# Hybrid decoder step: who loads the token forms at the passage from the up to the down projection, and when they are split

## The chip, the core and the metric

The kernel runs on one core of a Trainium2 chip. The metric is the time of one execution in microseconds (us), median of several runs; lower is better. TensorE multiplies matrices, VectorE (DVE) and ScalarE (ACT) do elementwise work, GpSimd (POOL) does some too, and SyncE (SP) only starts transfers. SP, ACT and POOL each have a queue of transfers (DMAs); all of them run on the same 16 DMA engines.

## The reference

One decoder layer for 592 token columns (16 meta tokens, 512 prompt tokens, 64 sample tokens). What matters here is the last step, a squared-ReLU MLP of width 8192 over a model width of 2048:

```
mix, c, sg, sh = token_mixer(rmsnorm(x), ...)
x = x + mix
u = relu(rmsnorm(x, norm2_w) @ w_up)      # (tokens, 2048) @ (2048, 8192)
x = x + (u * u) @ w_down                  # (tokens, 8192) @ (8192, 2048)
y = rmsnorm(x, final_norm_w)
```

All inputs and outputs are float32.

## The kernel before

The MLP works on 576 tokens as two halves of 288. Every block product of two by two is made with seven products instead of eight (a Strassen-like scheme), from sums of weight blocks and seven combinations of the activations, the *token forms* (`FORMS = 7`, numbered 0 to 6). Each operand is split into a high part (rounded) and a low part (the rest), and a product is 8 inner blocks times three matmuls: high by high, high weight by low form, low weight by high form. So one product is 24 matmuls of 128x128 by 288.

Seven products make a *pair*. There are 32 pairs of the up projection (`UP_PAIRS`, p = 0 to 31) and 32 of the down projection (p = 32 to 63). Below, (31,4) is product 4 of pair 31. Up pairs use token forms of x, down pairs use token forms of u*u, which the up pairs have made and stored, eight planes each, in DRAM (`u_forms`). Both live in the same buffers: `forms_a` holds forms 0 to 2, `forms_b` forms 3 to 6, each form a high and a low plane of 128 x 8 x 288. The passage is the replacement of the seven forms of x by the seven forms of the first eight up pairs, between pair 31 and pair 32. The buffer of form i is free when product (31,i), its last reader, has ended. After that 1.18 MB of it is loaded into the low plane (`load_form`), ACT rounds it into the high plane (`chunk_hi`, line 1728 of the profile), and DVE subtracts the high from the low plane in place, in two halves (`chunk_lo(i, half)`, line 2463).

Each engine runs its own instructions in the order written. DVE and ACT run through `slot(p, i)`, one slot for each product. A DVE slot takes the result of an earlier product (`take`, lines 2423 to 2445), makes the low part of the weights of product (p,i) (`mlp_lo`, line 2410, which waits until product i-2 has ended, since there are two buffers) and in some slots a weight sum (`weight_sum`, lines 2383, 2389, 2392, 2401) or forms of u (`u_forms`, lines 2452 to 2457); in the passage `chunk_lo` comes last in the slot. An ACT slot copies a result in slots 2 to 4 of up pairs (`copy_product`, line 1703), makes the high part of the weights of the next product (`mlp_hi`, line 1689), squares (`u_square`, line 1712), and in the passage does `chunk_hi` last. TensorE starts product (p,i) when `mlp_lo(p,i)` is done (`product_waits`); product (31,4) also waits for the copy of product (31,2); in pair 32 each product also waits for both halves of `chunk_lo(i)`.

Before the change SP's queue issues, in this order: weight blocks 128 to 130 (512 KB each; four blocks make a pair, block 4p + j), forms 0 and 1, blocks 131 and 132, form 2, the first tile of z (the running sum x that the down projection adds to, `load_z`), forms 3 and 4, block 133, forms 5 and 6. Each issue waits for its buffer and holds up those behind it. `weight_sum(32, 1)`, in DVE's slot (31,5), needs blocks 130 and 131. `load_z(32)` waits for POOL's store of the forms of pair 30 (`store_u(30)`), because z lies where they lay.

Of the kernel before, what the change touches and what calls it, by code (L numbers as in the profile page):

```python
# [21 lines left out]
F32 = mybir.dt.float32  # L22
F32R = mybir.dt.float32r
U8 = mybir.dt.uint8
ALU = mybir.AluOpType
ACT = mybir.ActivationFunctionType
# [29 lines left out]
KP = KT // 2  # L56
FORMS = 7
UP_PAIRS = DFF // P // 2
# [10 lines left out]
UB = [0, 1, 2, 4, 5, 6, 7]  # L69
# [14 lines left out]
F_ORDER = ([f"{i}_{k}" for k in range(KP - 1) for i in range(3)]  # L84
           + ["3a", "0_7", "1_7", "3b", "2_7", "4", "5a", "5b", "6"])
# [5 lines left out]
def unit_of(p, i):  # L91
    return MLP_U0 + FORMS * p + i
# [33 lines left out]


STEPS = PAIRS - UP_PAIRS
FIRST_FORMS = len(F_ORDER) + FORMS


def window(p):
# [4 lines left out]
def block_loads(n):  # L137

    p = n // 4
    return 2 if p >= UP_PAIRS and p - UP_PAIRS + KP > UP_PAIRS else 1  # L140


def block_count(n):

    return 16 * sum(block_loads(m) for m in range(n % BLOCKS, n + 1, BLOCKS))


def step_forms(t, group):

    return FIRST_FORMS + 2 * (t - 1) + 1 + group  # L150
# [83 lines left out]
def hymba_kernel(nc, io):  # L234
    ctx = ExitStack()
    with ctx:
# [160 lines left out]
        def form(i):  # L397

            f = forms_a[:, i] if i < 3 else forms_b[:, i - 3]
            return f[:, 0], f[:, 1]  # L400
# [46 lines left out]
        s_unit = sem("unit_done")  # L447
# [74 lines left out]
        def _(sp):  # L522
# [112 lines left out]
                    return  # L635
                sp.dma_start(wblock(n), src).then_inc(s_v[n % BLOCKS], 16)

            def load_form(i):

                sp.wait_ge(s_unit, unit_of(UP_PAIRS - 1, i) + 1)  # L640
                sp.wait_ge(s_ust[0], 16 * (KP // 2))
                sp.wait_ge(s_ust[1], 16 * (KP // 2))
                sp.dma_start(form(i)[1].bitcast(F32), u_dram[0:KP, UB[i]].rearrange("k p n -> p k n")).then_inc(s_fraw[i], 16)

            def load_z(p):
                d = p - UP_PAIRS
                if d < 2:
# [7 lines left out]
            for n in range(4 * PAIRS):  # L655
                load_block(n)
                p = n // 4 - 1 if n % 4 == 0 else PAIRS - 1 if n == 4 * PAIRS - 1 else 0
                for i in {4 * UP_PAIRS + 2: (0, 1), 4 * UP_PAIRS + 4: (2,)}.get(n, ()):
                    load_form(i)
                if p >= UP_PAIRS:  # L660
                    load_z(p)
                for i in {4 * UP_PAIRS + 4: (3, 4), 4 * UP_PAIRS + 5: (5, 6)}.get(n, ()):
                    load_form(i)

            sp.wait_ge(s_unit, unit_of(PAIRS - 1, 1) + 1)
            for r in range(2):
# [16 lines left out]
        def _(pool):  # L683
# [196 lines left out]
            def store_u(p):  # L880
                pool.wait_ge(s_uf, 3 * p + 3)
                pool.dma_start(u_dram[p].rearrange("f p n -> p f n"), ub[:, p % 2]).then_inc(s_ust[p % 2], 16)
# [14 lines left out]
                    pool.wait_ge(s_zf, 2 * e + 2)  # L897
                pool.dma_start(x1_dram[d % KP], z[:, p % 2]).then_inc(s_zst[p % 2], 16)

            for p in range(UP_PAIRS - 1):  # L900
                store_u(p)
            for p in range(UP_PAIRS - 1, PAIRS - 1):
                if p < UP_PAIRS:
                    store_u(p)
                else:
                    store_z(p)
# [46 lines left out]
        def _(pe):  # L953
# [331 lines left out]
            def part_product(p, i, ks):  # L1285

                f_hi, f_lo = form(i)
                u_ = unit_of(p, i)
                out = pbank(p, "abacaba"[i])
                t = p - UP_PAIRS  # L1290
                for k in ks:
                    if t > 0 and k == KP - 1 and i in (0, 3):
                        pe.wait_ge(s_flo, step_forms(t, i // 3))
                    if p == 0 and i < 3:
                        pe.wait_ge(s_flo, form_no(f"{i}_{k}"))
                    kx = k if t < 0 else window(p)[k] % KP
                    for n, (w, x) in enumerate(((hi_slot(u_), f_hi), (hi_slot(u_), f_lo), (w_lo[:, u_ % 2], f_hi))):
                        ins = mm(out, w[:, k, :], x[:, kx, :], start=i in (0, 1, 3) and k == 0 and n == 0,  # L1298
                                 stop=k == KP - 1 and n == 2, skip_group_check=True)
                    if k == KP - 1:  # L1300
                        ins.then_inc(s_unit, 1)

            def product_waits(p, i):
                pe.wait_ge(s_lo, unit_of(p, i) + 1)
                if i == 0:
                    if p < 2:
                        pe.wait_ge(s_evac, OUT_T0 + EARLY + KT - 1 + p)
                    else:
                        pe.wait_ge(s_ev, ev_end(p - 2))
                up = p < UP_PAIRS  # L1310
                if i == 2:
                    pe.wait_ge(s_tc, 3 * p + 1) if up else pe.wait_ge(s_ev, ev_no(p, 1))
                if i == 3 and p == 0:
                    pe.wait_ge(s_ws, 3)
                if i == 4:
                    pe.wait_ge(s_tc, 3 * p + 3) if up else pe.wait_ge(s_ev, ev_no(p, 3))
                if i == 6:
                    pe.wait_ge(s_ev, ev_no(p, 2 if up else 5))
                if p == UP_PAIRS:
                    pe.wait_ge(s_flo, len(F_ORDER) + i + 1)  # L1320
                if p == 0 and i >= 3:
                    pe.wait_ge(s_flo, form_no({3: "3b", 4: "4", 5: "5b", 6: "6"}[i]))

# [53 lines left out]
        def _(act):  # L1377
# [347 lines left out]
            def chunk_hi(i):  # L1725
                act.wait_ge(s_fraw[i], 16)
                f_hi, f_lo = form(i)
                A(f_hi, f_lo.bitcast(F32), ACT.Copy).then_inc(s_fhi, 1)

            def step_load(t, group):  # L1730

# [23 lines left out]
            def slot(p, i):  # L1755
                up = p < UP_PAIRS
                if up and 2 <= i <= 4:
                    copy_product(p, i - 2)
                if i < FORMS - 1:
                    mlp_hi(p, i + 1)  # L1760
                elif p + 1 < PAIRS:
                    mlp_hi(p + 1, 0)
                if p and i < 2:
                    if p - 1 < UP_PAIRS:
                        u_square(p - 1, i)
                    elif p - 1 >= PAIRS - KP:
                        z_finish(p - 1, i)
                t = p - UP_PAIRS
                if t == -1 and i >= 5:
                    chunk_hi(i - 5)  # L1770
                if t == 0 and i < 5:
                    chunk_hi(i + 2)
                if t == 0 and i == 4:
                    step_load(1, 0)
                if t == 0 and i == 6:
                    step_hi(1, 0)
                if t == 1 and i == 1:
                    step_load(1, 1)
                if t == 1 and i == 2:
                    step_hi(1, 1)  # L1780
                if t > 1 and i == 1:
                    step_hi(t, 1)
                if 0 < t < STEPS - 1:
                    if i == 0:
                        step_load(t + 1, 0)
                    if i == 3:
                        step_load(t + 1, 1)
                    if i == 4:
                        step_hi(t + 1, 0)
# [48 lines left out]
        def _(dve):  # L1838
# [620 lines left out]
            def chunk_lo(i, half):  # L2459
                f_hi, f_lo = form(i)  # L2460
                ks = slice(half * (KP // 2), (half + 1) * (KP // 2))
                dve.wait_ge(s_fhi, len(F_ORDER) + i + 1)
                ins = TT(f_lo[:, ks, :], f_lo[:, ks, :].bitcast(F32), f_hi[:, ks, :].bitcast(F32), ALU.subtract)  # L2463
                if half:
                    ins.then_inc(s_flo, 1)

            def step_lo(t, group):
                q = (t + KP - 1) % KP
# [6 lines left out]
            def slot(p, i):  # L2475
                if i >= 2:
                    take(p, i - 2)
                elif p:
                    take(p - 1, i + 5)
                mlp_lo(p, i)  # L2480
                if i == 1:
                    weight_sum(p, 3)
                if i == 3:
                    weight_sum(p, 4)
                if i >= 5 and p + 1 < PAIRS:
                    weight_sum(p + 1, i - 4)
                if 0 < p <= UP_PAIRS and i in (2, 4):
                    u_forms(p - 1, i // 2 - 1)
                t = p - UP_PAIRS
                if t == -1 and i == 6:  # L2490
                    chunk_lo(0, 0)
                if t == 0:
                    for f, half in {0: [(0, 1)], 1: [(1, 0), (1, 1)], 2: [(2, 0), (2, 1)], 3: [(3, 0), (3, 1)],
                                    4: [(4, 0), (4, 1)], 5: [(5, 0), (5, 1)], 6: [(6, 0), (6, 1)]}[i]:
                        chunk_lo(f, half)
                if t == 1 and i == 0:
                    step_lo(1, 0)
                if t == 1 and i == 3:
                    step_lo(1, 1)
                if t > 1 and i == 2:  # L2500
                    step_lo(t, 1)
                if 0 < t < STEPS - 1 and i == 4:
                    step_lo(t + 1, 0)
# [66 lines left out]
```

## Time and profile before

| | us |
|---|---|
| median of 3 runs | 2982.25 |
| lowest and highest | 2979.97, 2982.76 |
| the profiled execution | 2980.19 |
| its span, first to last instruction | 2978.1 |
| TensorE busy | 2899.3 (97%) |
| VectorE busy | 2055.7 (69%) |
| ScalarE busy | 1163.3 (39%) |
| mean granted TensorE clock | 0.991 of full |

The profile is one execution. Times in it are microseconds from the start of the span. A row of the timeline says when an instruction started, how long it took, its engine and line, and in brackets how long its engine had sat idle before it and who ended that. The time of an execution is 2.09 us more than its span. Two instructions of DVE or ACT overlap by about 0.1 us, so that the distance between starts is a little less than the duration.

### The profile page before, as it was taken

What the parts mean: (1) busy time and instruction counts of PE and PEld (TensorE: products, weight loads), DVE (VectorE), ACT (ScalarE), POOL (GpSimd) and SP (SyncE); (2) the same over time, 40 slices, a digit from 0 to 9 for tenths busy, and PEclk for the clock granted to TensorE, in tenths of its full rate; (3) what the DMA queues carried; (4) which work ended last, traced back from release to release, by engine and by line L of the source; (5) the groups of instructions that cost most, each with busy time, mean ns of one, the idle gap of its engine ahead of it and who ended that gap; (6) DMA issues with size and microseconds to landing.
All of it is one profiled execution on the core that took longest, in us unless ns stands there. A gap on an engine that the chain in (4) does not pass through costs nothing.

```text
span 2978.1 us, 51581 instructions
## 1 busy us (share of the span) xinstructions
PE 2899.3 (97%) x21544; PEld 2849.2 (96%) x21544; DVE 2055.7 (69%) x2868; ACT 1163.3 (39%) x1466; POOL 326.0 (11%) x480
## 2 busy tenths in 40 slices
PE   7999999999999999999999999999999999999998
PEld 7999999999999999999989999999998999999998
DVE  5556565757474747565477777777778887887885
ACT  5333333333332323333344444444444444444454
POOL 7211101010102020102100000000000000000111
PEclk9999999999999999999999999999999999999999
DMA  7344693333334523235335445445467666666665
GB/s 217 68 86 75 83 78 75 82 82 80 77 79 77 81 63 97 84 113 166 103 105 158 145 140 160 143 140 161 143 220 220 191 196 196 191 196 196 191 197 185
DMA packets 516471, 397.43 MB, mean 133 GB/s; under 512 B 16960, under 2 KB 484176, under 8 KB 516240
## 3 DMA queue, kind: packets, MB, share of 16 engines
q1 hardware_dynamic: 462272, 268.86, 38.1%
q0 software_dynamic: 22896, 88.43, 8.0%
q10 hardware_dynamic: 31072, 36.85, 4.1%
q8 instruction: 170, 2.79, 0.4%
q14 instruction: 61, 0.50, 0.1%
HBM read 309.72 MB, written 84.37 MB: 132 GB/s over the span
## 4 chain that ended last, share of the span: by engine, by line
PE 86%; DVE 9%; ACT 2%; issue 2%; DMA 1%; SPq 0%; POOL 0%; ACTq 0%; DVEq 0%; POOLq 0%
PE main L1298 40%; PE main L961 29%; PE mx L1298 7%; PE mx L1198 2%; DVE w_lo L1845 1%; PE mx L1097 1%; PE mx L1105 1%; PE mx L1021 1%; DVE w_lo L2410 1%; ACT w_hi L1386 0%; PE mx L1205 0%; DVE tmp L2008 0%; PE mx L1139 0%; PE mx L1215 0%; ACT tmp L1477 0%
## 5 line engine op out<-in xcount | busy, mean ns | idle before, releaser
L1298 PE MATMUL main<-forms_b,w_hi 128*128 128x288 f32 x3072 | 616.7, 296 | 10.0 <-DVE w_lo L2410 4.7
L1298 PE MATMUL main<-forms_a,w_hi 128*128 128x288 f32 x3072 | 616.7, 296 | 6.3 <-DVE forms_a L2463 4.7
L961 PE MATMUL main<-h_hi,w_hi 128*128 128x296 f32 (+1 forms) x2592 | 609.2, 316 | 13.4 <-DVE w_lo L1845 12.4
L961 PE MATMUL main<-h_hi,w_lo 128*128 128x296 f32 (+1 forms) x2592 | 565.8, 300 | 0.0
L961 PE MATMUL main<-h_lo,w_hi 128*128 128x296 f32 (+1 forms) x2592 | 565.7, 300 | 0.0
L1298 PEld LDWEIGHTS main<-forms_b,w_hi 128*128 128x128 f32 x3072 | 494.4, 189 | 11.5 <-DVE w_lo L2410 7.5
L1298 PEld LDWEIGHTS main<-forms_a,w_hi 128*128 128x128 f32 x3072 | 495.9, 189 | 7.9 <-issue 5.1
L1298 PE MATMUL main<-forms_a,w_lo 128*128 128x288 f32 x1536 | 455.7, 297 | 0.0
L1298 PE MATMUL main<-forms_b,w_lo 128*128 128x288 f32 x1536 | 453.7, 295 | 0.0
L961 PEld LDWEIGHTS main<-h_hi,w_hi 128*128 128x128 f32 x2592 | 417.3, 191 | 29.1 <-DVE w_lo L1845 17.3
L961 PEld LDWEIGHTS main<-h_lo,w_hi 128*128 128x128 f32 x2592 | 423.2, 190 | 0.0
L961 PEld LDWEIGHTS main<-h_hi,w_lo 128*128 128x128 f32 x2592 | 422.9, 190 | 0.0
L1689 ACT ACTIVATE w_hi<-w_raw 128x1024 fp32r<-128x1024 f32 x256 | 271.2, 1060 | 326.7 <-PE main L1298 223.5
L2410 DVE TENSOR_TENSOR w_lo<-w_raw,w_hi 128x1024 fp32r<-128x1024 f32 x256 | 312.4, 1220 | 65.3 <-PE main L1298 65.3
L1689 ACT ACTIVATE w_hi<-w_sum 128x1024 fp32r<-128x1024 f32 x190 | 201.6, 1061 | 299.6 <-PE main L1298 295.3
L1298 PEld LDWEIGHTS main<-forms_b,w_lo 128*128 128x128 f32 x1536 | 290.5, 189 | 0.0
L1298 PEld LDWEIGHTS main<-forms_a,w_lo 128*128 128x128 f32 x1536 | 289.7, 189 | 0.0
L1845 DVE TENSOR_TENSOR w_lo<-w_raw,w_hi 128x1024 fp32r<-128x1024 f32 x162 | 199.1, 1229 | 101.5 <-ACT w_hi L1386 101.4
L1386 ACT ACTIVATE w_hi<-w_raw 128x1024 fp32r<-128x1024 f32 x162 | 170.5, 1053 | 246.6 <-PE main L961 233.1
L2410 DVE TENSOR_TENSOR w_lo<-w_sum,w_hi 128x1024 fp32r<-128x1024 f32 x190 | 234.1, 1232 | 16.9 <-PE main L1298 16.9
L1298 PE MATMUL mx<-forms_b,w_hi 128*128 128x288 f32 x1024 | 207.0, 296 | 1.9 <-DVE forms_b L2463 1.7
L2423 DVE TENSOR_TENSOR z<-z,main 128x288 f32<-128x288 f32 x192 | 87.2, 454 | 120.4 <-PE main L1298 120.3
(389 smaller groups left out, 3530.7 us busy)
## 6 DMA issues: line engine op xcount, KB each, us to landing
w_raw<-in_w_in SPq DMA_DIRECT2D x130, 512.0 KB, 7.6
w_raw<-in_w_up SPq DMA_DIRECT2D x128, 512.0 KB, 4.1
w_raw<-in_w_down SPq DMA_DIRECT2D x100, 512.0 KB, 4.7
u_forms<-ub POOLq DMA_DIRECT2D x32, 1152.0 KB, 6.9
z<-x_scratch SPq DMA_DIRECT2D x32, 576.0 KB, 7.5
x_scratch<-z POOLq DMA_DIRECT2D x31, 576.0 KB, 3.1
stage<-u_forms ACTq DMA_DIRECT2D x30, 576.0 KB, 4.0
w_raw<-in_w_out SPq DMA_DIRECT2D x32, 512.0 KB, 4.0
```

Of the source, the lines that this page charges most:

```text
L961: ins = mm(out[:, half, :], w[:, ring, k, :], x[:, kx, half * width:half * width + width], start=first and n == 0, stop=last_ and n == 2)
L1021: ins = mm(mx[:, i + half, 0:HALF], ones[:, :], src[:, half * HALF:half * HALF + HALF], start=True, stop=True)
L1097: ins = mm(bank(0, 64 * c, 64), xl[:, c, :], left, start=True, stop=True)
L1105: ins = mm(bank(1, 64 * c, 64), tT[:, c, :], pc[:, c, :], start=True, stop=True)
L1198: ins = mm(bank(i % 2, 64 * c, 64, n_), win(hkk, c, n_), right, start=True, stop=True)
L1298: ins = mm(out, w[:, k, :], x[:, kx, :], start=i in (0, 1, 3) and k == 0 and n == 0, stop=k == KP - 1 and n == 2, skip_group_check=True)
L1386: A(w_hi[:, ring % 2], w_raw[:, ring], ACT.Copy).then_inc(s_hi, 1)
L1689: A(hi_slot(u_), src, ACT.Copy).then_inc(s_hi, 1)
L1845: TT(w_lo[:, ring % 2], w_raw[:, ring], w_hi[:, ring % 2].bitcast(F32), ALU.subtract).then_inc(s_lo, 1)
L2410: TT(w_lo[:, u_ % 2], src, hi_slot(u_).bitcast(F32), ALU.subtract).then_inc(s_lo, 1)
L2423: TT(o[:, q, :], o[:, q, :], src, ALU.add).then_inc(s_ev, 1)
```

## The change

Four things change, all in the passage.

1. The seven form loads leave SP's queue and go to POOL's: forms 0 to 2 between the stores of pairs 29 and 30, forms 3 to 6 between the stores of pairs 30 and 31. Each still waits for its own product of pair 31.
2. ACT makes the high part in two halves (1152 elements for each partition, not 2304), and in slots (31,3) to (32,2), not (31,5) to (32,4).
3. DVE's 14 halves stand in slots (31,4) to (32,5), not (31,6) to (32,6): one in (31,4), two each in (31,5) to (32,2), one each in (32,3) to (32,5), and they may run after the half that they need.
4. TensorE waits for the first half of form i before product (32,i), and for the second in the middle of it.

```diff
-FIRST_FORMS = len(F_ORDER) + FORMS
+FIRST_FORMS = len(F_ORDER) + 2 * FORMS
+def first_half(i, half):
+    return len(F_ORDER) + 2 * i + half + 1
 # SP
-            def load_form(i):
-                sp.wait_ge(s_unit, unit_of(UP_PAIRS - 1, i) + 1)
...
-                for i in {4 * UP_PAIRS + 2: (0, 1), 4 * UP_PAIRS + 4: (2,)}.get(n, ()):
-                    load_form(i)
...
-                for i in {4 * UP_PAIRS + 4: (3, 4), 4 * UP_PAIRS + 5: (5, 6)}.get(n, ()):
-                    load_form(i)
 # POOL
+            def load_form(i):
+                pool.wait_ge(s_unit, unit_of(UP_PAIRS - 1, i) + 1)
...
+                pool.dma_start(form(i)[1].bitcast(F32), u_dram[0:KP, UB[i]].rearrange("k p n -> p k n")).then_inc(s_fraw[i], 16)
-            for p in range(UP_PAIRS - 1):
+            for p in range(UP_PAIRS - 2):
                 store_u(p)
+            for i in range(3):
+                load_form(i)
+            store_u(UP_PAIRS - 2)
+            for i in range(3, FORMS):
+                load_form(i)
 # TensorE
+                    if t == 0 and k == KP // 2:
+                        pe.wait_ge(s_flo, first_half(i, 1))
...
-                    pe.wait_ge(s_flo, len(F_ORDER) + i + 1)
+                    pe.wait_ge(s_flo, first_half(i, 0))
 # ACT
-                A(f_hi, f_lo.bitcast(F32), ACT.Copy).then_inc(s_fhi, 1)
+                for half in range(2):
+                    ks = slice(half * (KP // 2), (half + 1) * (KP // 2))
+                    A(f_hi[:, ks, :], f_lo[:, ks, :].bitcast(F32), ACT.Copy).then_inc(s_fhi, 1)
...
-                if t == -1 and i >= 5:
-                    chunk_hi(i - 5)
-                if t == 0 and i < 5:
-                    chunk_hi(i + 2)
+                if t == -1 and i >= 3:
+                    chunk_hi(i - 3)
+                if t == 0 and i < 3:
+                    chunk_hi(i + 4)
 # DVE
-                if t == -1 and i == 6:
-                    chunk_lo(0, 0)
-                if t == 0:
-                    for f, half in {0: [(0, 1)], 1: [(1, 0), (1, 1)], ...}[i]:
-                        chunk_lo(f, half)
+                if t in (-1, 0):
+                    n0, n1 = {4: (0, 1), 5: (1, 3), 6: (3, 5)}.get(i, (0, 0)) if t else ((5, 7), (7, 9), (9, 11), (11, 12), (12, 13), (13, 14), (14, 14))[i]
+                    for n in range(n0, n1):
+                        chunk_lo(n // 2, n % 2)
```

On POOL, from the last stores of up pairs on, this stands before the change (`u_forms<-ub` is the store of a pair's forms, `x_scratch<-z` a store of z):

```order
L872 TENSOR_TENSOR sq_sum<-sq_sum,sq 128x576
L882 DMA u_forms<-ub 128x8x288 x32
L898 DMA x_scratch<-z 128x1152 x24
L893 COPY rstd<-part 128x576
L896 TENSOR_TENSOR rstd<-rstd,part 128x576
```

and this after it, where `forms_a<-u_forms` and `forms_b<-u_forms` are the form loads:

```order
L876 DMA u_forms<-ub 128x8x288 x30
L899 DMA forms_a<-u_forms 128x8x288 x3
L876 DMA u_forms<-ub 128x8x288
L899 DMA forms_b<-u_forms 128x8x288 x4
L876 DMA u_forms<-ub 128x8x288
```

The form loads now stand among the stores of POOL's queue, on which nothing else goes in this stretch.

On SP's queue, this stands from the last up blocks on, before the change (`w_raw<-in_w_down` are weight blocks of the down projection, from 128 on):

```order
L636 DMA w_raw<-in_w_up 128x8x128 x128
L633 DMA w_raw<-in_w_down 128x8x128 x3
L643 DMA forms_a<-u_forms 128x8x288 x2
L633 DMA w_raw<-in_w_down 128x8x128 x2
L643 DMA forms_a<-u_forms 128x8x288
L653 DMA z<-x_scratch 128x1152
L643 DMA forms_b<-u_forms 128x8x288 x2
L633 DMA w_raw<-in_w_down 128x8x128
L643 DMA forms_b<-u_forms 128x8x288 x2
L633 DMA w_raw<-in_w_down 128x8x128 x3
```

and this after it:

```order
L641 DMA w_raw<-in_w_up 128x8x128 x128
L638 DMA w_raw<-in_w_down 128x8x128 x5
L651 DMA z<-x_scratch 128x1152
L638 DMA w_raw<-in_w_down 128x8x128 x4
L651 DMA z<-x_scratch 128x1152
```

Blocks 130 and 131 follow each other directly, and z follows block 132.

On DVE, from the end of slot (31,4) to the start of slot (32,0), this stands before the change (`part` is a result being taken, `w_lo` the weights' low part, `w_sum` a weight sum, `forms_a<-forms_a` a half of a form):

```order
L2457 TENSOR_TENSOR ub<-ub 128x288
L2430 TENSOR_TENSOR part<-part,mx 128x288
L2410 TENSOR_TENSOR w_lo<-w_sum,w_hi 128x1024
L2383 TENSOR_TENSOR w_sum<-w_raw 128x1024
L2433 TENSOR_TENSOR part<-part,main 128x288
L2410 TENSOR_TENSOR w_lo<-w_raw,w_hi 128x1024
L2389 TENSOR_TENSOR w_sum<-w_sum,w_raw 128x1024
L2463 TENSOR_TENSOR forms_a<-forms_a 128x1152
L2436 TENSOR_TENSOR part<-part,main 128x288
```

and this after it:

```order
L2467 TENSOR_TENSOR ub<-ub 128x288
L2473 TENSOR_TENSOR forms_a<-forms_a 128x1152
L2440 TENSOR_TENSOR part<-part,mx 128x288
L2420 TENSOR_TENSOR w_lo<-w_sum,w_hi 128x1024
L2393 TENSOR_TENSOR w_sum<-w_raw 128x1024
L2473 TENSOR_TENSOR forms_a<-forms_a 128x1152 x2
L2443 TENSOR_TENSOR part<-part,main 128x288
L2420 TENSOR_TENSOR w_lo<-w_raw,w_hi 128x1024
L2399 TENSOR_TENSOR w_sum<-w_sum,w_raw 128x1024
L2473 TENSOR_TENSOR forms_a<-forms_a 128x1152 x2
L2446 TENSOR_TENSOR part<-part,main 128x288
```

Five halves stand where one stood.

## Rows read from the trace of the kernel before

**Rows 1.** Whom TensorE waited for, 2175 to 2300 us: total, times, longest.

```profile
PE main L1298 <- DVE forms_a L2463: 4.7, 2, 3.0
PE main L1298 <- DVE forms_b L2463: 3.4, 3, 1.8
PE mx L1298 <- DVE forms_b L2463: 1.7, 1, 1.7
PE main L1298 <- DVE w_lo L2410: 1.2, 1, 1.2
```

**Rows 2.** Timeline of TensorE: first matmuls of (31,0), (32,6), (33,0), (34,0).

```profile
2200.96 0.42 PE L1298 MATMUL main<-forms_a,w_hi 128*128 128x288 f32 x2
...
2259.36 0.50 PE L1298 MATMUL main<-forms_b,w_hi 128*128 128x288 f32 x2 [0.22 <-DVE forms_b L2463]
...
2262.60 0.43 PE L1298 MATMUL main<-forms_a,w_hi 128*128 128x288 f32 x2
...
2284.93 0.42 PE L1298 MATMUL main<-forms_a,w_hi 128*128 128x288 f32 x2
```

**Rows 3.** Timeline of VectorE in the passage: start, us, instruction, idle before.

```profile
2213.89 0.45 DVE L2430 TENSOR_TENSOR part<-part,mx 128x288 f32<-128x288 f32 x1 [1.03 <-PE mx L1298]
...
2218.66 1.22 DVE L2383 TENSOR_TENSOR w_sum<-w_raw 128x1024 f32<-128x1024 f32 x1 [3.18 <-issue]
2219.80 0.45 DVE L2433 TENSOR_TENSOR part<-part,main 128x288 f32<-128x288 f32 x1
2220.16 1.22 DVE L2410 TENSOR_TENSOR w_lo<-w_raw,w_hi 128x1024 fp32r<-128x1024 f32 x1
2221.30 1.22 DVE L2389 TENSOR_TENSOR w_sum<-w_sum,w_raw 128x1024 f32<-128x1024 f32 x1
2222.43 1.35 DVE L2463 TENSOR_TENSOR forms_a<-forms_a 128x1152 fp32r<-128x1152 f32 x1
...
2234.00 0.45 DVE L2423 TENSOR_TENSOR z<-z,main 128x288 f32<-128x288 f32 x1 [1.11 <-PE main L1298]
...
2254.32 1.22 DVE L2410 TENSOR_TENSOR w_lo<-w_raw,w_hi 128x1024 fp32r<-128x1024 f32 x1
2255.46 1.22 DVE L2389 TENSOR_TENSOR w_sum<-w_sum,w_raw 128x1024 f32<-128x1024 f32 x1
2256.59 2.62 DVE L2463 TENSOR_TENSOR forms_b<-forms_b 128x1152 fp32r<-128x1152 f32 x2
```

**Rows 4.** SP's queue: start and us of issues.

```profile
2204.39 3.47 SPq L643 DMA_DIRECT2D forms_a<-u_forms  x2
2209.96 3.75 SPq L633 DMA_DIRECT2D w_raw<-in_w_down  x2
...
2222.32 0.34 SPq L653 DMA_DIRECT2D z<-x_scratch  x1
```

**Rows 5.** Issue to landing: form 0 (2204.39), block 131 (2209.96), z (2222.32); KB, us.

```profile
forms_a<-u_forms SPq DMA_DIRECT2D x1, 1152.0 KB, 9.2
...
w_raw<-in_w_down SPq DMA_DIRECT2D x1, 512.0 KB, 8.6
...
z<-x_scratch SPq DMA_DIRECT2D x1, 576.0 KB, 5.4
```

**Rows 6.** Stretches of 2 us: busy times, granted clock, DMA share, GB/s.

```profile
2228.00:2230.00 2.00, 2.00 (x9) 2.00 (x10) 2.00 (x3) 1.89 (x3) 0.00 (x0) 0.50 1.08 391
...
2242.00:2244.00 2.00, 0.37 (x3) 0.13 (x1) 2.00 (x3) 1.54 (x2) 0.00 (x0) 1.00 0.43 122
```

**Rows 7.** POOL's and ScalarE's timelines: a store of forms, the split of form 2.

```profile
2213.16 0.89 POOL L882 DMA_DIRECT2D u_forms<-ub  x1 [20.98 <-DVE ub L2457]
...
2226.24 2.12 ACT L1728 ACTIVATE forms_a<-forms_a 128x2304 fp32r<-128x2304 f32 x1 [0.58 <-DMA forms_a<-u_forms]
```

**Rows 8.** DMA queues 2218.5 to 2220 us (q0 POOL, q1 SP): packets, MB, share.

```profile
q0 software_dynamic: 125, 0.58, 101.6%
q1 hardware_dynamic: 24, 0.01, 2.7%
```

More of the change, by code:

```diff
@@ L636, in load_block @@
                 sp.dma_start(wblock(n), src).then_inc(s_v[n % BLOCKS], 16)
-            def load_form(i):
-                sp.wait_ge(s_unit, unit_of(UP_PAIRS - 1, i) + 1)
-                sp.wait_ge(s_ust[0], 16 * (KP // 2))
-                sp.wait_ge(s_ust[1], 16 * (KP // 2))
-                sp.dma_start(form(i)[1].bitcast(F32), u_dram[0:KP, UB[i]].rearrange("k p n -> p k n")).then_inc(s_fraw[i], 16)
             def load_z(p):
@@ L898, in store_z @@
                 pool.dma_start(x1_dram[d % KP], z[:, p % 2]).then_inc(s_zst[p % 2], 16)
-            for p in range(UP_PAIRS - 1):
-                store_u(p)
+            def load_form(i):
+                pool.wait_ge(s_unit, unit_of(UP_PAIRS - 1, i) + 1)
+                pool.wait_ge(s_ust[0], 16 * (KP // 2))
+                pool.wait_ge(s_ust[1], 16 * (KP // 2))
+                pool.dma_start(form(i)[1].bitcast(F32), u_dram[0:KP, UB[i]].rearrange("k p n -> p k n")).then_inc(s_fraw[i], 16)
+            for p in range(UP_PAIRS - 2):
+                store_u(p)
+            for i in range(3):
[3 more added lines that the diff above has]
+                load_form(i)
             for p in range(UP_PAIRS - 1, PAIRS - 1):
@@ L2461, in chunk_lo @@
                 ks = slice(half * (KP // 2), (half + 1) * (KP // 2))
[L2462 to L2465, printed above, removed]
+                dve.wait_ge(s_fhi, first_half(i, half))
+                TT(f_lo[:, ks, :], f_lo[:, ks, :].bitcast(F32), f_hi[:, ks, :].bitcast(F32), ALU.subtract).then_inc(s_flo, 1)
             def step_lo(t, group):
@@ L2489, in slot @@
                 t = p - UP_PAIRS
-                if t == -1 and i == 6:
-                    chunk_lo(0, 0)
-                if t == 0:
-                    for f, half in {0: [(0, 1)], 1: [(1, 0), (1, 1)], 2: [(2, 0), (2, 1)], 3: [(3, 0), (3, 1)],
-                                    4: [(4, 0), (4, 1)], 5: [(5, 0), (5, 1)], 6: [(6, 0), (6, 1)]}[i]:
-                        chunk_lo(f, half)
+                if t in (-1, 0):
+                    n0, n1 = {4: (0, 1), 5: (1, 3), 6: (3, 5)}.get(i, (0, 0)) if t else ((5, 7), (7, 9), (9, 11), (11, 12), (12, 13), (13, 14), (14, 14))[i]
+                    for n in range(n0, n1):
+                        chunk_lo(n // 2, n % 2)
                 if t == 1 and i == 0:
```

## The prediction

> **What bounds the kernel now.** TensorE is busy 97% of the span, so only the places where it stops can give time. The view of who waited for whom, cut to the passage, comes first: TensorE stood 4.7 + 3.4 + 1.7 + 1.2 = 11.0 us, all behind DVE [rows 1]. The timeline of TensorE then says what the passage costs. From (33,0) to (34,0), an ordinary pair, 22.33 us pass; from (31,0) to (33,0), two pairs, 61.64 [rows 2], which is 17.0 more than 44.66. The rest beyond the 11.0 is TensorE at half clock: the stretch from 2228 shows a granted clock of 0.50, its lower level of 1.2 GHz, after the longest stop of 3.0 us [rows 6, 1].
>
> Does TensorE's slowness cost time here? DVE's timeline decides. From 2212.9 to 2259.2 it has only three gaps: 1.03 us before 2213.89, 3.18 before 2218.66, 1.11 before 2234.00 [rows 3]. So DVE sets the pace: its slot is 0.36 for a take, 1.14 for the low part, often 1.13 for a weight sum (distances of starts at 2219.80, 2220.16, 2221.30, 2222.43 [rows 3]), and 1.27 for a half of a form (2.62 for two less 1.35 [rows 3]), while TensorE needs 22.33 / 7 = 3.19 a product. Two halves in a slot make about 5.2 with a sum, 4.0 without. The 14 halves are 17.8 us of DVE work for which pairs leave only some room.
>
> The gap of 3.18 is the wait of `weight_sum(32,1)` for block 131: issued at 2209.96, landed 8.6 later, at 2218.56 [rows 4, 5], behind forms 0 and 1 on SP's queue. The DMA engines are full meanwhile: 391 GB/s at 2228, and down to 122 only at 2242 [rows 6].
>
> **The change, part by part.** It removes no DVE work. ACT gets seven more instructions; its split takes 2.12 whole [rows 7], about 2.2 in two halves, and ACT is 39% busy over the span: nothing, unless it waits. What can be won is DVE's idle time and the tail.
>
> *Idle.* Slot (31,4) gets a half where DVE idled 1.03. Block 131 no longer stands behind two forms on its queue: at best the 3.18 go. The 1.11 came from product (32,0) at half clock, taken in slot (32,2); with two more halves ahead of it there DVE has work instead. Sum 5.32.
>
> *Tail.* Before, (32,6) waits for its own two halves: low part started 2254.32, ended 2255.5, then a sum of 1.13 and 2.54 of halves, TensorE at 2259.36 [rows 2, 3]. Now all 14 halves stand ahead of that low part, and the product starts when it ends: the halves cost the same, the sum and the 0.2 after the last half leave the path: 1.3.
>
> The bound is 5.32 + 1.3 = 6.7 us. With it (33,0) would start near 2256. What is next to be late is TensorE itself.
>
> *What is given back: data.* In the new order DVE reaches `weight_sum(32,1)` at 2212.86 + 1.27 + 0.36 + 1.14 = 2215.6. Block 131 is still issued near 2210, when its buffer is free, and shares full DMA engines with forms 0 and 1, due at the same moments as before. If it lands where it did, at 2218.56, DVE idles 3.0; if it loses only the wait on its own queue, some 2 us earlier, 0.9. I take 1.7, since the engines are full either way. Form 0 bites in the same amount: it landed 9.2 after 2204.39, at 2213.6 [rows 4, 5]; ACT now stands before it in slot (31,3), and queued behind that on ACT are the copy of product (31,2), for which (31,4) waits, and the high parts for (31,5). Landing at 2213.6 plus 2.2 and 0.4 would start (31,4) at 2216.2, not at 2200.96 + 4 x 3.19 = 2213.7. POOL issues at once at 2204.1, in 0.89 us [rows 7], and form 0 is no longer behind block 130, so I expect 2211 to 2212.5. The two delays lie beside each other, so 1.7 counts once; bounds 0 and 3.0.
>
> *Given back: clock.* The stop of about 3 us before (32,0) stays (DVE has four halves more to do by then, TensorE the same pace), so a fall to 0.50 follows it again, hidden behind DVE. A second fall, late, when DVE has one half a slot left, is not hidden: a stretch of 3.4 us at half clock costs at most 1.7. I take 1.0; bounds 0 and 1.7.
>
> Each POOL issue waits for a product in order, and the store of pair 30 stands behind form 2, which waits for (31,2), ended at 2200.96 + 3 x 3.19 = 2210.5; the store came at 2213.16 anyway [rows 7]: nothing. Form 3 follows it by 0.89: nothing. The new wait of TensorE in mid-product: halves are at least a slot ahead: nothing.
>
> Sum: 6.7 - 1.7 - 1.0 = 4.0 us faster. The profiled execution would be 2980.19 - 4.0 = 2976.2 (its span is 2.09 less). It lies 2.06 under the median of the runs, so the forecast is 2982.25 - 4.0 = 2978.2.
>
> **Rivals.**
> *All data in time* (6.7 faster, 2975.6). For it: forms 0 and 1 now bring nothing in front of block 131 on its queue, and SP's blocks have small needs. Against it: 391 GB/s is the most the engines show, and bytes are the same.
>
> *z comes late* (1 faster, 2981.3). `load_z(32)` waits for the store of pair 30, which landed before 2222.32 and z 5.4 after that, at 2227.7 [rows 4, 5]. Now that store is behind form 2 in POOL's queue, and z, on SP's, may stand behind forms 4 to 6, which are now issued as products (31,4) to (31,6) end; 1.18 MB at 391 GB/s are 3.0 us each, so z could land at 2225 + 5.4 + 9 = 2239.4. DVE wants it near 2236: 3.4 of the 4.0 go, with some of form 3's lateness to ACT in the same place. Against it: only 0.6 MB, and on another queue than the forms.
>
> *Block 131 is starved* (slower). Between 2218.5 and 2220 the store of POOL moved 125 packets of 4.6 KB while SP's queue moved 24 of 512 B [rows 8]. If an engine takes one packet from each queue in turn, a POOL packet takes 16 x 1.5 / 125 = 0.19 us, and a block, 1024 packets or 64 an engine, needs 64 x 0.22 = 14 us as long as POOL's queue is full. It now is, from 2206 to past 2226, since a form comes every 3.2 us. Block 131 would land at 2226, DVE would idle 10.4 instead of the 0 of the bound: 6.7 - 10.4 = 3.7 slower, 2986.0. The change is slower from a landing of 2215.6 + 6.7 = 2222.3 on. Against it: SP's form 2 may simply not have been under way in that stretch, so the small share of q1 can be lack of work, and the block would be served in its place. The Trainium skill, "DMA: Bandwidth & Descriptors", section on queues, rings and completion order, says that each DMA engine goes round its queues and changes at packet boundaries only; by that rule this rival is the outcome. The row's 125 to 24 agrees with it and does not prove it.
>
> **How the numbers follow.** The forecast (2 to 6 faster, 2976.2 to 2980.2) has 0.50, all in time 0.20, z late 0.18, the starved block 0.12. A measurement of this kernel tells 0.2%, 6.0 us, from no change. Faster by more than that: most of the second case and the edge of the first, 0.25. Slower by more: only a block still later than 2228, 0.05. The rest, 0.70, is within. The range leaves out a tenth at each end: from 2975.2 (the bound and a little) to 2984.5 (part of the starved block).
>
> **What would show it.** DVE's gap before `weight_sum(32,1)` at 0.9 to 3 us, none of 1 us in slot (31,4); TensorE's (32,6) starting right after its low part; from (31,0) to (33,0) 57 to 58 us instead of 61.64; stops of TensorE in pair 32 behind the weights' low part and no longer behind the forms; block 131's landing between 2216 and 2219. A landing past 2222, POOL's packets crowding SP's, makes the forecast wrong; so do an ACT that idles over 2 us before a split with TensorE stopped after it, or a wait of DVE's first z take.

## The result and the profile after

| | before | after |
|---|---|---|
| median of 20 runs each, us | 2980.54 | 2985.49 |
| lowest and highest | 2977.79, 2984.05 | 2981.15, 2989.95 |
| ratio after to before, 95% interval | | 1.0016 (1.0010 to 1.0022) |
| span of the profiled execution | 2978.1 | 2983.1 |
| from (31,0) to (33,0) | 61.64 | 67.33 |
| from (33,0) to (34,0) | 22.33 | 22.35 |

By the medians the change made the kernel 4.95 us slower, by the interval of the ratio 3.0 to 6.6. The forecast was 4.0 us faster. The whole loss lies in the two pairs of the passage, which is where [rows 2] put the place to look. TensorE's timeline of the changed kernel, first matmuls of (31,0), (33,0) and (34,0):

```profile
2200.86 0.29 PE L1306 MATMUL main<-forms_a,w_hi 128*128 128x288 f32 x1
...
2268.19 0.43 PE L1306 MATMUL main<-forms_a,w_hi 128*128 128x288 f32 x2
...
2290.54 0.42 PE L1306 MATMUL main<-forms_a,w_hi 128*128 128x288 f32 x2
```

Whom TensorE waited for in the changed kernel, 2175 to 2300 us (total, times, longest), to be set against [rows 1]:

```profile
PE main L1306 <- DVE w_lo L2420: 13.8, 7, 9.1
PE main L1306 <- ACT part L1711: 2.2, 1, 2.2
PE mx L1306 <- DVE w_lo L2420: 1.2, 1, 1.2
```

The stops are 17.2 us, where there were 11.0. None is behind a form any more, as was forecast; one stop of 9.1 is new, and its releaser is a low part of weights. That is only the messenger. DVE's timeline in the changed kernel names what DVE itself waited for, and answers to [rows 3]:

```profile
2214.46 1.36 DVE L2473 TENSOR_TENSOR forms_a<-forms_a 128x1152 fp32r<-128x1152 f32 x1 [1.70 <-ACT forms_a L1738]
2215.74 0.45 DVE L2440 TENSOR_TENSOR part<-part,mx 128x288 f32<-128x288 f32 x1
2216.76 1.22 DVE L2420 TENSOR_TENSOR w_lo<-w_sum,w_hi 128x1024 fp32r<-128x1024 f32 x1 [0.57 <-ACT w_hi L1697]
2227.87 1.23 DVE L2393 TENSOR_TENSOR w_sum<-w_raw 128x1024 f32<-128x1024 f32 x1 [9.89 <-DMA w_raw<-in_w_down]
2229.02 2.62 DVE L2473 TENSOR_TENSOR forms_a<-forms_a 128x1152 fp32r<-128x1152 f32 x2
...
2271.61 0.45 DVE L2433 TENSOR_TENSOR z<-z,main 128x288 f32<-128x288 f32 x1 [0.50 <-PE main L1306]
```

DVE waited 9.89 us for block 131 (3.18 before), and worked after it without a gap until 2271. Its idle time in the passage is 1.70 + 0.57 + 9.89 = 12.16 us; before it was 5.32. The time from issue to landing of block 131 went from 8.6 us [rows 5] to 17.9:

```profile
w_raw<-in_w_down SPq DMA_DIRECT2D x1, 512.0 KB, 17.9
```

Why a load of 512 KB needs that long stands in the view of the DMA queues of the changed kernel (packets, MB, share of the 16 engines), here for four stretches: 2210 to 2212 us, 2214 to 2215, 2216 to 2217, and 2220 to 2224:

```profile
q0 software_dynamic: 172, 0.73, 104.1%
...
q1 hardware_dynamic: 414, 0.21, 73.9%
q0 software_dynamic: 29, 0.11, 30.8%
...
q0 software_dynamic: 67, 0.30, 88.0%
q1 hardware_dynamic: 84, 0.04, 16.5%
...
q0 software_dynamic: 330, 1.43, 90.3%
q1 hardware_dynamic: 332, 0.17, 14.1%
```

Read these four stretches as a story. First POOL's queue (q0) has the engines alone, with forms 0 and 1. Block 131 is issued at 2209.86, but its first packet starts at 2213.51: from 2210 to 2213 q0 moves 249 packets and SP's queue (q1) none. That is not one for one, and no run here says why; in the kernel before, the block's first packet came 3.96 us after its issue, behind the forms on one queue. Then form 1 runs out and form 2 has not begun, and block 131 gets a hole: 414 of its 1024 packets in one microsecond. From 2216 form 2, the store of pair 30 and form 3 follow one another on q0, and in four microseconds q0 moves 330 packets (311 of 4608 B and 19 of 4 B) and q1 332 of 512 B, of blocks 131 and 132. From here on it is one packet for one packet, and q1 gets an eighth of q0's bytes. The trace's landings of block 131 show both: on 9 of the 16 engines it had landed by 2216.8, after the hole; on the last four it landed between 2224.8 and 2227.8. From the shares, a round of one packet from each queue takes 4 x 16 x (0.903 / 330 + 0.141 / 332) = 0.20 us on an engine; by this estimate the 64 packets of an engine that finds no hole take 12.9 us.

TensorE's clock follows the stop and costs little, since DVE has the pace. Two stretches of the changed kernel (busy times of PE, PEld, DVE, ACT and POOL; then granted clock, DMA share, GB/s):

```profile
2224.00:2226.00 2.00, 0.06 (x1) 0.00 (x0) 0.00 (x0) 0.01 (x1) 0.88 (x1) 1.00 1.04 392
...
2228.00:2230.00 2.00, 0.00 (x0) 0.00 (x0) 2.00 (x2) 2.00 (x3) 0.00 (x0) 0.50 1.06 385
```

In the first, the compute engines stand (POOL only issues a load) while the DMA engines move 392 GB/s. Hardly any of it is what DVE waits for: in these 2 us q1 moved 0.08 of 0.78 MB, and block 131 was still under way on four engines at most.

### The profile page after: what moved, and what is told of

Read it like the earlier page. It is cut to its first block, busy times and chain, and to the rows that moved or that the text cites. A ratio compares the mean times of both kernels' runs of the same rounds, so it can differ in the third digit from the quotient of the medians.

```text
span 2983.1 us, 51588 instructions
## 1 busy us (share of the span) xinstructions
PE 2898.3 (97%) x21544; PEld 2847.4 (95%) x21544; DVE 2056.0 (69%) x2868; ACT 1163.3 (39%) x1473; POOL 331.7 (11%) x487
## 4 chain that ended last, share of the span: by engine, by line
PE 85%; DVE 9%; ACT 2%; issue 2%; DMA 1%; POOL 0%; SPq 0%; DVEq 0%; POOLq 0%; ACTq 0%
PE main L1306 40%; PE main L967 29%; PE mx L1306 7%; PE mx L1204 2%; DVE w_lo L1855 1%; PE mx L1103 1%; PE mx L1111 1%; PE mx L1027 1%; DMA w_raw<-in_w_down 1%; ACT w_hi L1394 0%; PE mx L1211 0%; DVE tmp L2018 0%; PE mx L1145 0%; DVE w_lo L2420 0%; PE mx L1221 0%
## 5 line engine op out<-in xcount | busy, mean ns | idle before, releaser
L1306 PE MATMUL main<-forms_b,w_hi 128*128 128x288 f32 x3072 | 618.5, 296 | 17.7 <-DVE w_lo L2420 13.7
L1306 PEld LDWEIGHTS main<-forms_b,w_hi 128*128 128x128 f32 x3072 | 495.8, 189 | 19.5 <-DVE w_lo L2420 17.2
L967 PEld LDWEIGHTS main<-h_hi,w_hi 128*128 128x128 f32 x2592 | 417.3, 191 | 29.5 <-DVE w_lo L1855 17.7
```

The lines of the kernel that those rows point to most:

```text
L967: ins = mm(out[:, half, :], w[:, ring, k, :], x[:, kx, half * width:half * width + width], start=first and n == 0, stop=last_ and n == 2)
```

## The experiments

All were timed in five rounds beside the kernel before, whose median was 2980.76 to 2981.41 us in these sets. After the result there were two theories. *Starved*: block 131 is late because POOL's packets alternate with its own. *Schedule*: the new places of the halves cost the time, by putting ACT and DVE behind forms that have not landed.

**The schedule alone, and the queue alone.** The first kernel is the changed one with the form loads back on SP's queue:

```diff
 # SP
+                for i in {4 * UP_PAIRS + 2: (0, 1), 4 * UP_PAIRS + 4: (2,)}.get(n, ()):
+                    load_form(i)
...
 # POOL
-            for i in range(3):
-                load_form(i)
...
```

> The changed kernel with the form loads put back on SP's queue, in the places they had before; the new order of the splits on ScalarE and VectorE and the new waits of TensorE stay. Theory S (block 131 of the down weights is starved by GpSimd's transfers, one packet for one packet): all landings go back to those of before (block 131 at 2218.6, form 0 at 2213.6, form 2 at 2226.2), VectorE idles about 3 us before weight_sum(32,1) and not 9.9; walking the engines' rows with these landings puts product (33,0) 2.7 us earlier than in the kernel before: 2977.8 where before is 2980.5. Theory H (the new order itself costs, since ScalarE now stands before form 0 and holds up the copy for product (31,4), and the halves stand ahead of more products): slower than before by most of the 4.9 us, 2984 to 2985.

The second is the kernel before, with only the loads on POOL's queue:

```diff
 # SP
-                for i in {4 * UP_PAIRS + 2: (0, 1), 4 * UP_PAIRS + 4: (2,)}.get(n, ()):
-                    load_form(i)
...
 # POOL
+            for i in range(3):
+                load_form(i)
...
```

> The kernel before with the form loads moved to GpSimd's queue as in the change, nothing else. Theory S: block 131 lands at 2226 to 2228, VectorE idles 10 to 12 us before weight_sum(32,1), and since the old order keeps its tail the time is worse than that of the changed kernel: the walk gives 7.8 us slower than before, 2988.3. Theory H: the queue is harmless, the time is that of before or up to 1.5 us less (forms land earlier), 2979 to 2980.5.

Measured: 2977.52 us, ratio 0.9988 (0.9979 to 0.9997), and 2991.50 us, ratio 1.0032 (1.0019 to 1.0044). The second has five runs only, and its profile is of the fastest of them, 2985.59 us; its passage took 69.58 us, 7.9 more than before, which is what was expected, while the median is 3.2 us above the 2988.3 expected. No trace of a run near the median was kept, so where the rest went is open. DVE's gaps of over 1 us in the slots of form 0 and of block 131, of the schedule alone:

```profile
2214.81 1.36 DVE L2472 TENSOR_TENSOR forms_a<-forms_a 128x1152 fp32r<-128x1152 f32 x1 [1.58 <-ACT forms_a L1737]
...
2218.72 1.22 DVE L2392 TENSOR_TENSOR w_sum<-w_raw 128x1024 f32<-128x1024 f32 x1 [0.39 <-DMA w_raw<-in_w_down]
```

and of the queue alone:

```profile
2226.65 1.22 DVE L2384 TENSOR_TENSOR w_sum<-w_raw 128x1024 f32<-128x1024 f32 x1 [12.32 <-issue]
```

with its DMA queues from 2220 to 2224 us:

```profile
q0 software_dynamic: 326, 1.43, 90.2%
q1 hardware_dynamic: 322, 0.16, 13.6%
```

The schedule alone gains and the queue alone loses, and the same one for one stands in a kernel that has none of the new schedule. So *Schedule* falls as the reason for the loss. A part of it stays: in the schedule alone DVE still waits 1.58 us before its first half, since form 0 has not landed, and that is idle time which the new places did not remove.

**Dose.** If form 2's packets are what meets the block, holding form 2 back must free it, and holding only form 3 must leave it to form 2 and the store.

```diff
             for i in range(3):
+                if i == 2:
+                    pool.wait_ge(s_v[(4 * UP_PAIRS + 3) % BLOCKS], block_count(4 * UP_PAIRS + 3))
                 load_form(i)
```

> The changed kernel, but GpSimd issues the load of form 2 only when block 131 has landed; nothing else differs. Theory S: block 131 shares the engines with forms 0 and 1 only, lands at about 2217.5 and not at 2227.8, VectorE's wait falls from 9.9 to 1 to 2 us; form 2 lands about 2 us later, which its split can bear. Time 4 us below the kernel before, 2976 to 2977.5. Theory H: form 2, the store of pair 30 and forms 3 to 6 all come later, so the time is that of the changed kernel or worse, 2985 to 2988.

Measured: 2980.27 us, ratio 0.9995 (0.9986 to 1.0004). DVE waited 0.76 us for the block:

```profile
2217.94 1.22 DVE L2395 TENSOR_TENSOR w_sum<-w_raw 128x1024 f32<-128x1024 f32 x1 [0.76 <-DMA w_raw<-in_w_down]
```

The wait for the block came out as expected; the time missed by some 3 us. Form 2, expected 2 us later than in the changed kernel, landed 5.3 later (counted from (31,0)); DVE had gaps of 0.82 and 0.76 us before halves of forms 2 and 3, and pair 33 took 23.08 us and not 22.33. The same wait before form 3 instead:

> The changed kernel, but GpSimd issues form 3 (and all behind it) only when block 131 has landed. Theory S: block 131 shares its engines one for one with forms 1 and 2 and the store of pair 30, which last to about 2223, then runs alone: last landing 2223.5 to 2225, between 2217.9 (form 2 held) and 2227.8 (nothing held). VectorE waits about 6 us. The walk gives 1.5 us slower than before: 2982 to 2983. If the landing stays at 2228, the delay does not come from what stands in GpSimd's queue.

Measured: 2985.01 us, ratio 1.0014 (1.0005 to 1.0023).

```profile
2225.38 1.23 DVE L2395 TENSOR_TENSOR w_sum<-w_raw 128x1024 f32<-128x1024 f32 x1 [6.26 <-DMA w_raw<-in_w_down]
```

Its DMA queues, 2218 to 2222 us, where form 2 and the store still run, and 2224 to 2225, where they have all but ended:

```profile
q0 software_dynamic: 304, 1.33, 91.6%
q1 hardware_dynamic: 304, 0.15, 13.9%
...
q1 hardware_dynamic: 439, 0.22, 72.5%
q0 software_dynamic: 13, 0.04, 9.5%
```

The wait is 0.76, 6.26 and 9.89 us with form 2, form 3 and nothing held. Here too pair 33 stretched (23.38 us), which is 1.0 of the 2 to 3 us that the time lies above what was expected.

**One issue moved.** The strictest test leaves all bytes and all form loads as they are, and only gives block 131 its place inside POOL's queue, between forms 1 and 2:

```diff
 # SP
-                load_block(n)
+                if n != 4 * UP_PAIRS + 3:
+                    load_block(n)
...
 # POOL
+            def load_block_3():
+                n = 4 * UP_PAIRS + 3
+                pool.wait_ge(s_ws, 4 * ((n - BLOCKS) // 4) + 4)
+                pool.dma_start(wblock(n), w_down[:, 1:2 * KP:2, P:2 * P]).then_inc(s_vp, 16)
...
             for i in range(3):
+                if i == 2:
+                    load_block_3()
                 load_form(i)
...
```

> The changed kernel, with one transfer moved: block 131 is issued by POOL, between forms 1 and 2, and not by SP. All bytes and all seven form loads stay as they are. If sharing the engines one packet for one packet with form 2, the store and form 3 is what starves it, it now has its place inside one queue, ahead of form 2: its 64 packets of 512 B an engine take 64 x 0.027 = 1.7 us after form 1's end, so it lands between 2217 and 2219, DVE waits for it 0.3 to 2 us and not 9.9, the two pairs take 58.8 to 60.5 us and not 67.3, and the time is 2.4 to 0.5 us under before, 2978 to 2980. The rival that the engines are simply full of bytes at that point has the landing stay past 2224 and the time near 2985. A third: writing 1024 small packets costs POOL's queue as much per packet as 256 large ones, so the block's packets come late and form 2 behind them; then the landing is 2220 to 2224 and the time about that of before.

Measured: 2976.77 us, ratio 0.9983 (0.9974 to 0.9992). The passage took 58.20 us, 9.1 less than in the changed kernel. DVE's wait for the block:

```profile
2219.26 1.23 DVE L2408 TENSOR_TENSOR w_sum<-w_raw 128x1024 f32<-128x1024 f32 x1 [0.55 <-DMA w_raw<-in_w_down]
```

POOL's timeline, the block at 2210.60 and form 2 right behind it, and the DMA queues from 2214 to 2216 us:

```profile
2210.60 0.88 POOL L906 DMA_DIRECT2D w_raw<-in_w_down  x1 [1.58 <-DVE w_sum L2426]
2211.48 0.88 POOL L901 DMA_DIRECT2D forms_a<-u_forms  x1
```

```profile
q0 software_dynamic: 170, 0.63, 102.9%
```

The engines were just as full (102.9%), so full engines are not the cause; who shares them with whom is. The third theory falls too: the block landed 17.9 us after the start of (31,0), in time, and form 2 landed 1.5 us later than in the changed kernel. Note that two things changed for the block: its place, and its packets, which were 4096 B on POOL's queue and not 512. This run does not say how much each of them gave.

**The loads on ACT's queue.** 

```diff
+                if t == -1 and i >= 2:
+                    load_form(i - 2)      # ACT
+                if t == 0 and i < 2:
+                    load_form(i + 5)
```

> The changed kernel with the seven form loads issued from ScalarE's queue, one in each of its slots (31,2) to (32,1), all else as in the change. The loads are again on another queue than block 131, but in packets of 1152 B (0.05 us each) and not 4.6 KB (0.19 us). Theory S, one packet for one packet: block 131's 64 packets an engine now wait 64 x 0.05 us, about 3 to 5 us in all, not 12 to 17; it lands at 2216 to 2218.5, VectorE's wait for it falls from 9.9 to under 3 us, and the time is 2 to 4 us below the kernel before: 2977 to 2979. Theory Q (any second queue beside SP's delays block 131 as much, whatever the packets): landing near 2228 and 2985 again.

Measured: 2979.21 us, ratio 0.9998 (0.9990 to 1.0007); the passage took 60.17 us. DVE's wait for the block was short:

```profile
2223.78 1.23 DVE L2392 TENSOR_TENSOR w_sum<-w_raw 128x1024 f32<-128x1024 f32 x1 [1.48 <-DMA w_raw<-in_w_down]
```

But this time does not settle the part that the size of a packet plays. The form loads stood behind ACT's own work there, and from 2218 to 2222 us the form queue (q10) had hardly anything under way:

```profile
q1 hardware_dynamic: 1820, 0.92, 89.6%
q0 software_dynamic: 50, 0.23, 15.7%
q10 hardware_dynamic: 134, 0.14, 11.4%
```

A later stretch of this trace shows the rule with other sizes. From 2222.5 to 2224 POOL's store and a form on ACT's queue were both under way: 101 packets of q0 in 0.47 MB, 104 of q10 in 0.12 MB. With rows of 1152 B, one for one leaves the smaller packets a quarter of the bytes of the larger, and not an eighth.

**SP's order.** All loads on SP, in the order form 0, block 131, forms 1 to 3, block 132, form 4, z, form 5, block 133, form 6.

> The new split order, all form loads on SP's queue, but in another order there: form 0, block 131, forms 1, 2, 3, block 132, form 4, the first z tile, form 5, block 133, form 6 (before: forms 0, 1, blocks 131, 132, form 2, z, forms 3, 4, block 133, forms 5, 6). Theory S, with first come first served on one queue: block 131 stands behind form 0 alone and lands at about 2215.5, VectorE does not wait for it, form 1 lands at about 2218; the walk gives 4.9 us faster than before, 2975.6. Theory H: no better than e1_split_only, slower than before.

Measured: 2980.65 us, ratio 0.9999 (0.9990 to 1.0008). A miss: counted from (31,0), the block landed 1.2 us earlier than before, but form 1 6.6 us later, and the largest gap moved there:

```profile
2222.70 1.36 DVE L2470 TENSOR_TENSOR forms_a<-forms_a 128x1152 fp32r<-128x1152 f32 x1 [4.17 <-ACT forms_a L1735]
```

The block ahead of form 1 had been priced by its bytes. The rest stands in the trace: form 1 now ran beside the store of pair 30 on POOL's queue, and from 2216.5 to 2218 q0 moved 104 packets (0.48 MB) and q1, with the rows of form 1, 117 (0.13 MB). That is the same sharing, with a form as the one that suffers; no run without the store beside it was made.

**The halves placed by the landings.** With the loads on SP, ACT's splits start one slot later and DVE's halves stand where their forms had landed in the schedule alone (the loads as there, not shown again):

```diff
-                    n0, n1 = {4: (0, 1), 5: (1, 3), 6: (3, 5)}.get(i, (0, 0)) if t else ((5, 7), (7, 9), (9, 11), (11, 12), (12, 13), (13, 14), (14, 14))[i]
+                    n0, n1 = {4: (0, 2), 6: (2, 3)}.get(i, (0, 0)) if t else ((3, 5), (5, 7), (7, 9), (9, 11), (11, 13), (13, 14), (14, 14))[i]
...
```

> Loads on SP's queue in the order of the kernel before (as e1_split_only), but the splits placed by the landings that the traces show: ScalarE's halves one slot later, (31,4) to (32,3), behind the copy that product (31,4) waits for; VectorE's halves two in (31,4), none in (31,5), one in (31,6), two each in (32,0) to (32,4), one in (32,5). VectorE then has two halves to do while block 131 is under way (landing 2218.6), and TensorE no longer stops before (31,4). The walk gives 4.9 us faster than before, 2.2 better than e1_split_only: 2975.8. If the gain of e1_split_only comes only from the tail and not from the idle time, it stays at 2977.5.

Measured: 2976.51 us, ratio 0.9989 (0.9981 to 0.9998). One gap of DVE was left:

```profile
2215.96 2.63 DVE L2472 TENSOR_TENSOR forms_a<-forms_a 128x1152 fp32r<-128x1152 f32 x2 [2.16 <-ACT forms_a L1737]
```

The same with forms 2 to 5 and z ahead of block 132 on SP's queue:

> As e7_fill_wait, and SP's order is: block 130, forms 0, 1, block 131, forms 2, 3, 4, the first z tile, form 5, block 132, form 6, block 133. Blocks 132 and 133 are not needed before pair 33, so nothing should wait for them; forms 2 and 3 should land up to 2 us earlier. The walk gives the same 4.9 us as e7_fill_wait, since its halves of form 2 are not late; a loss against it would mean that the store of pair 30, on GpSimd's queue, or z now delays a form.

Measured: 2975.39 us, ratio 0.9982 (0.9973 to 0.9991). And these halves with block 131 on POOL's queue:

> The kernel of the block on POOL's queue, with ACT's and DVE's halves placed as in the version that put them by the landings (ACT from slot (31,4), DVE two halves in (31,4), none in (31,5), one in (31,6)). If the loads on POOL's queue are as good as SP's once the block has its place, DVE's only gap is the one before form 0 (about 2 us), the two pairs take 57.2 to 58.5 us, and the time is 3 to 4.5 us under before, 2976.5 to 2978. If the queue itself costs something more (late packets, late form 2), the gap before the weight sum returns and the time stays over 2979.

Measured: 2975.98 us, ratio 0.9982 (0.9974 to 0.9991). By the medians the three beat the kernel before by 4.4, 5.6 and 5.4 us (by the intervals at least 0.6, 2.7 and 2.7) and the changed one by 9 to 10; the intervals do not tell them apart. The last gap, before form 0, is in all of them.

**All of them in one table.** Idle is DVE's, between the end of slot (31,3) and (33,0), summed over the gaps in brackets of its timeline. The 6.7 is the bound of the prediction. Gain is how much shorter the passage is than 61.64 us. The landing of the block is that on its last engine, counted from the start of (31,0); in the kernel before it was 17.6.

| kernel | block 131 lands | DVE waits for it | idle | 6.7 - idle | gain seen | median, us |
|---|---|---|---|---|---|---|
| changed kernel | 26.9 | 9.89 | 12.16 | -5.5 | -5.7 | 2985.49 |
| form 3 held | 23.6 | 6.26 | 8.81 | -2.1 | -2.3 | 2985.01 |
| SP's order | 16.4 | 0 | 6.75 | -0.1 | -0.3 | 2980.65 |
| form 2 held | 17.9 | 0.76 | 4.95 | 1.8 | 1.3 | 2980.27 |
| ACT's queue | 19.1 | 1.48 | 4.64 | 2.1 | 1.5 | 2979.21 |
| schedule alone | 17.3 | 0.39 | 3.52 | 3.2 | 2.9 | 2977.52 |
| block on POOL's queue | 17.9 | 0.55 | 3.09 | 3.6 | 3.4 | 2976.77 |
| halves by the landings | 17.7 | 0 | 2.16 | 4.5 | 4.4 | 2976.51 |
| the same, block on POOL | 18.2 | 0.44 | 2.24 | 4.5 | 4.4 | 2975.98 |
| the same, SP's second order | 17.7 | 0 | 2.10 | 4.6 | 4.4 | 2975.39 |

The queue alone has the old order of halves, and so no share in the tail of 1.3: its block landed at 26.8, its idle was 13.36, 5.32 - 13.36 gives -8.0, and -7.9 was seen.

## Why the prediction was wrong

**The step that failed** is "given back: data", taken at 1.7 us within 0 and 3.0. It was 9.89 + 0.57 + 1.70 = 12.16 us, against 5.32 of idle that were to go, so that 6.7 - 12.16 = -5.5 was left, and -5.7 was seen. It took the landing of block 131 as bounded above by where it stood before, 2218.56, because "the engines are full either way". That a queue which no longer stands ahead of the block can hold it up more than one that did was left to a rival at 0.12. The loads left SP's queue, where they would have stood *behind* the block (forms 2 to 6), and went to one where they stood *beside* it, at nine times its bytes a packet. A second part of this step failed too: the delay by form 0 and that by the block were taken to lie beside each other and counted once. In the changed kernel they add up, 1.70 + 0.57 in front of the 9.89; in the schedule alone they are 1.58 + 0.57 in front of 0.39.

**How the rival was weighed.** The starved block was forecast to land at 2226, with 10.4 us of idle and 2986.0 us; seen were 2227.8, 9.89 and 2985.5. The mechanism was right; that the time fits so well is in part luck. The rival meant 3.7 us slower than a median of 2982.25, and measured was 4.95 slower than one of 2980.54; and DVE came to the block 2.4 us later than reckoned, which hid that the block was 1.8 later. I held against it that 24 packets of SP in [rows 8] might be lack of work. They were in part: block 131 had landed by 2218.56, and block 132 on 13 engines by 2218.9. On the last three engines block 132 was still under way, and there the trace of the kernel before already shows the rule: its packets start at 2218.92, 2218.95 and 2219.00, then at 2219.13, 2219.15 and 2219.20, at 2219.33, 2219.36 and 2219.40, that is three packets in every 0.20 us for three engines, and a POOL packet takes 0.19 to 0.20. So the row spoke for the rival, and was counted as if it spoke against. The Trainium skill, "DMA: Bandwidth & Descriptors", section on queues, rings and completion order, has each engine go round its queues, changing at packet boundaries; the changed trace agrees from 2216 on, with 330 packets to 332, and does not from 2210 to 2213, with 249 to none while block 131 was already issued. What the rival had not seen is the hole between forms 1 and 2. It let 9 of the 16 engines finish by 2216.8, and did not help, as a block is there when its last engine is.

**The bound was right.** Idle of 5.32 and a tail of 1.3 made 6.7 us. The table shows it in ten kernels: 6.7 less DVE's idle gives the gain of the passage within 0.6 us, and within 0.3 in eight of them. So DVE does set the pace. The tail shows by itself too: (32,6) started 1.28 us after the start of its low part, without its sum and halves in front, where it had taken 5.04 (of the 3.76 between them 2.54 are halves that now stand earlier):

```profile
2263.60 1.22 DVE L2420 TENSOR_TENSOR w_lo<-w_raw,w_hi 128x1024 fp32r<-128x1024 f32 x1
...
2264.88 0.53 PE L1306 MATMUL main<-forms_b,w_hi 128*128 128x288 f32 x2 [0.44 <-DVE w_lo L2420]
```

**Given back to the clock** was 1.0 us within 0 and 1.7. The gains seen lie under 6.7 less idle by 0.1 to 0.6 us, and by 0.2 in the changed kernel; that remainder holds whatever the clock took. It was over-sized, and its event did not come: the second, late fall to half clock stands in the kernel before (granted clock 0.60 and 0.54 in the stretches of 2 us from 2254), while in the changed kernel the clock is 1.00 from 2240 to 2268.

**Form 0** was expected at 2211 to 2212.5 and landed at 2213.2, 0.4 earlier than before and not 1 to 2.6. It no longer stood behind block 130 on a queue, but its first packet started at 2206.86, 2.3 us after its issue at 2204.52. For most of that time the engines were not full: from 2204.5 to 2206.5 q1 moved block 130 with 56% of them, and q0 nothing. In the kernel before its first packet had started at 2207.38, so 0.5 us was all that the other queue gave. ACT waited for it before its first split, 2213.26 in its timeline, which is one of the signs of being wrong that the prediction named (an ACT that idles over 2 us before a split, with TensorE stopped after it):

```profile
2213.26 2.22 ACT L1738 ACTIVATE forms_a<-forms_a 128x1152 fp32r<-128x1152 f32 x2 [4.50 <-DMA forms_a<-u_forms]
2215.39 0.39 ACT L1711 ACTIVATE part<-main 128x288 f32<-128x288 f32 x1
```

The copy behind it is the one that TensorE then waited 2.2 us for. That chain was foreseen (2216.2 as its worst case), and the 1.58 and 2.16 us of the kernels with SP's loads show that it costs about the same on either queue.

**z late** did not show: z was issued at 2224.1 and landed at 2236.8, 9 us later than before, but DVE had by then been held up more by the block. In the kernel with block 131 on POOL's queue z landed at 2234.3 and no gap of DVE stood before its first take. (The 391 GB/s that the prediction calls the most the engines show is not quite that: the kernel before has 397 in the stretch from 2218.)

## What to carry to other kernels

Before moving a bulk transfer to another queue, list the small urgent transfers that were ahead of it or behind it on the old one: on one queue order protects them, on two nothing does but the number and size of packets. Ask for each whether its packets are smaller than those of the newcomer; here 512 B against 4.6 KB left the block's queue an eighth of the other's bytes and made 8.6 us into 17.9. If the bulk must move, move the urgent transfer with it, ahead of the part that would crowd it: that one issue was worth 9 us here.

## What the runs showed of the hardware

- Once both have packets under way, two queues share the DMA engines by packets and not by bytes: 330 to 332 and 326 to 322 in 4 us, 304 to 304 in another kernel; with rows of 1152 B as the smaller ones, 101 to 104 and 104 to 117 in 1.5 us.
- An issued transfer need not have packets under way. With POOL's queue full, block 131's first packet started 3.65 us after its issue, and q1 moved none from 2210 to 2213. Why is open.
- The size of a packet depends on the queue. The same block of 512 KB went in 1024 packets of 512 B from SP's queue and in packets of 4096 B from POOL's. The forms' rows of 1152 B went as packets of 4608 B from POOL's queue and as 1152 B from ACT's.
- The last engine sets a landing. Block 131 was there on the ninth of 16 engines at 2216.8 and on the last at 2227.8; a mean rate of the transfer says nothing of when it can be used.
- Full engines by themselves did not delay the block: with POOL's queue alone at 102.9% it was in time.
